# Differential attention: another order of each engine's work within a head, and the last input tile of the output projection behind two weight chunks

## What is computed

```python
def diff_mixer(xn, k, v, w_q, q_gain, lam_params, head_gain, w_out, lambda_init):
    q = rms_norm((xn @ w_q).reshape(B, S, DIFF_HEADS, 2, DIFF_DH), q_gain) * (DIFF_DH ** -0.5)
    lam = jnp.exp(jnp.sum(lp[0] * lp[1])) - jnp.exp(jnp.sum(lp[2] * lp[3])) + lambda_init
    ...
        s = jnp.where(kpos[None, :] <= qpos[:, None], s, -jnp.inf)
        p = jax.nn.softmax(s, axis=-1)
        a = p[:, :, 0] - lam * p[:, :, 1]
        return jnp.einsum('bhqk,bhkv->bhqv', a.astype(v.dtype), v)
    ...
    o = rms_norm(o, head_gain) * (1.0 - lambda_init)
    return o.reshape(B, S, DIFF_HEADS * DIFF_VD) @ w_out
```

## Time and profile before

| | us |
|---|---|
| median of 3 runs | 2490.27 |
| lowest and highest | 2487.11, 2493.24 |
| the profiled execution | 2492.17 |
| its span in the trace | 2490.4 |
| mean granted clock of TensorE, share of full | 0.985 |
| TensorE busy with matmuls | 2395.2 (96% of the span) |
| VectorE busy | 1124.2 (45%) |
| ScalarE busy | 894.8 (36%) |

### The profile page before, as it was taken

One profiled execution on the slowest core, in us unless ns is written; L12 is line 12 of the kernel. 1 busy time (PEld: TensorE's weight loads), 2 busy tenths in 40 slices (PEclk: granted clock), 3 DMA queues, 4 the chain that ended last, 5 costly groups with the idle time before them and its releaser, 6 DMA issues.

```text
span 2490.4 us, 27086 instructions
## 1 busy us (share of the span) xinstructions
PE 2395.2 (96%) x11160; PEld 1928.4 (77%) x11160; DVE 1124.2 (45%) x1744; ACT 894.8 (36%) x1416; POOL 0.2 (0%) x4
## 2 busy tenths in 40 slices
PE   8889999999999999999999889999999997999999
PEld 7556788888877788888788768888887665888887
DVE  4444444344365444344556644324443554542342
ACT  4544332122255322223433433213333664431331
POOL 0000000000000000000000000000000000000000
PEclk9999999999999999999999989999999998999999
DMA  3111222322211222322221112222222110222222
GB/s 128 53 51 68 72 98 83 111 102 79 83 57 62 85 102 87 108 102 82 89 80 60 60 51 97 90 102 102 90 103 85 51 34 34 102 102 86 100 102 85
DMA packets 35579, 206.58 MB, mean 83 GB/s; under 512 B 4080, under 2 KB 4976, under 8 KB 16000
## 3 DMA queue, kind: packets, MB, share of 16 engines
q1 hardware_dynamic: 33120, 199.43, 23.4%
q10 hardware_dynamic: 2336, 5.41, 0.6%
HBM read 202.73 MB, written 2.10 MB: 82 GB/s over the span
## 4 chain that ended last, share of the span: by engine, by line
PE 92%; DVE 4%; ACT 2%; issue 2%; DMA 1%; DVEq 0%; SPq 0%; ACTq 0%
PE ps L285 27%; PE ps L287 27%; PE ps L286 27%; PE ps L980 2%; PE ps L1024 1%; PE ps L1020 1%; PE ps L1890 1%; PE ps L1535 1%; DVE low_w L311 1%; PE ps L1004 1%; PE ps L1871 1%; PE ps L991 1%; DVE diff_p L2097 0%; PE ps L1856 0%; DMA raw_w<-in_w_a_qk 0%
## 5 line engine op out<-in xcount | busy, mean ns | idle before, releaser
L285 PE MATMUL ps<-xh,high_w 128*128 128x512 f32 x1592 | 635.8, 399 | 12.2 <-DVE low_w L330 9.4
L286 PE MATMUL ps<-xl,high_w 128*128 128x512 f32 x1592 | 624.2, 392 | 0.0
L287 PE MATMUL ps<-xh,low_w 128*128 128x512 f32 x1592 | 624.2, 392 | 0.0
L311 DVE TENSOR_TENSOR low_w<-raw_w,high_w 128x2048 fp32r<-128x2048 f32 (+3 forms) x209 | 424.9, 2035 | 204.5 <-ACT high_w L303 204.2
L303 ACT ACTIVATE high_w<-raw_w 128x2048 fp32r<-128x2048 f32 (+3 forms) x209 | 355.2, 1702 | 298.4 <-PE ps L287 281.4
L285 PEld LDWEIGHTS ps<-xh,high_w 128*128 128x128 f32 x1592 | 301.7, 189 | 89.4 <-issue 25.2
L287 PEld LDWEIGHTS ps<-xh,low_w 128*128 128x128 f32 x1592 | 301.4, 189 | 64.3
L286 PEld LDWEIGHTS ps<-xl,high_w 128*128 128x128 f32 x1592 | 301.7, 189 | 61.9 <-issue 1.2
L285 PE MATMUL ps<-ffn_hidh,high_w 128*128 128x512 f32 x864 | 336.1, 389 | 0.0
L286 PE MATMUL ps<-ffn_hidl,high_w 128*128 128x512 f32 x864 | 336.1, 389 | 0.0
L287 PE MATMUL ps<-ffn_hidh,low_w 128*128 128x512 f32 x864 | 336.1, 389 | 0.0
(11 more groups left out here) (241 smaller groups left out, 2581.5 us busy)
## 6 DMA issues: line engine op xcount, KB each, us to landing
raw_w<-in_w_f_gu SPq DMA_DIRECT2D x44, 1024.0 KB, 4.9
raw_w<-in_w_m_up SPq DMA_DIRECT2D x32, 1024.0 KB, 4.9
raw_w<-in_w_m_dn SPq DMA_DIRECT2D x32, 1024.0 KB, 4.9
raw_w<-in_w_f_dn SPq DMA_DIRECT2D x32, 704.0 KB, 4.1
raw_w<-in_w_b_qk SPq DMA_DIRECT2D x8, 1024.0 KB, 4.9
raw_w<-in_w_e_qk SPq DMA_DIRECT2D x4, 1024.0 KB, 4.9
raw_w<-in_w_e_out SPq DMA_DIRECT2D x4, 1024.0 KB, 4.9
raw_w<-in_w_o_q SPq DMA_DIRECT2D x8, 512.0 KB, 3.6
```

The lines of the kernel that those rows point to most:

```text
L285: pe.matmul(out, sh, mh, start=start, stop=False)
L286: pe.matmul(out, sh, ml, start=False, stop=False)
L287: return pe.matmul(out, sl, mh, start=False, stop=stop)
L311: dve.tensor_tensor(wl[slot][:, 0:elems], raw[slot][:, 0:elems], wh[slot][:, 0:elems].bitcast(F32), ALU.subtract).then_inc(w_split, 1)
```

## The change

It changes the order of instructions on TensorE, ScalarE and VectorE within the steps and the tail of the differential attention. `F_BANK` and the counts that go with it are changed. `resid_pe` gets a parameter `late`: with 1, the input tiles 0 to 6 are taken through chunks 0 and 1, and the last tile then through both. Three input tiles of chunk 0 move into head 7's step. On VectorE the masks are cut in two groups with the weight split and the scaling of the next head's Q between them.

```diff
--- before.py
+++ after.py
@@ -604,21 +604,32 @@
         wait_for(pe, R.ready, max(1, k + 1 - R.before))
         return resid_tile(pe, R, c, k)
-    def resid_pe(pe, R, done=0, between={}):
-        def one(c, n):
+    def resid_pe(pe, R, done=0, late=0, between={}):
+        def go(n, k):
+            between.get((n, k), lambda: None)()
             if n == 0:
-                for k in range(done, R.kt):
-                    between.get(k, lambda: None)()
-                    last = resid_first(pe, R, k)
+                last = resid_first(pe, R, k)
             else:
-                pe.wait_ge(w_split, c + 1)
-                banks_read(pe, R, n)
-                for k in range(R.kt):
-                    last = resid_tile(pe, R, c, k)
-            last.then_inc(w_used, 1)
-        each_chunk(R.st, one)
+                if k == 0:
+                    pe.wait_ge(w_split, R.st.base + n + 1)
+                    banks_read(pe, R, n)
+                last = resid_tile(pe, R, R.st.base + n, k)
+            if k == R.kt - 1:
+                last.then_inc(w_used, 1)
+        order = [(0, k) for k in range(done, R.kt)]
+        if late:
+            cut = R.kt - late
+            order = ([(0, k) for k in range(done, cut)] + [(1, k) for k in range(cut)]
+                     + [(0, k) for k in range(cut, R.kt)] + [(1, k) for k in range(cut, R.kt)])
+        for n, k in order:
+            go(n, k)
+        for n in range(2 if late else 1, R.st.count):
+            for k in range(R.kt):
+                go(n, k)
     def resid_act(act, R):
@@ -1763,7 +1774,7 @@
     H = sems("hn", "squared summed logged rooted scaled rounded split")
     NHD = 8
     FQ, FK = (f_q0, f_q1), (f_k0, f_k1)
-    F_BANK = (2, 3, 4, 5, 6, 2, 3, 4)
+    F_BANK = (5, 6, 2, 3, 4, 2, 3, 4)
     def f_probs(buf, i):
         return f_p[:, buf, CAUSAL_AT[i]:CAUSAL_AT[i + 1]]
@@ -1866,7 +1877,7 @@
             for i in rows_of:
                 for hh in range(2):
                     n = 2 * i + hh
-                    wait_past(pe, F["masked"], 8 * p + n - 4 if n > 4 else 8 * (p - 1) + min(n + 6, 8))
+                    wait_past(pe, F["masked"], 8 * p + n - 2 if n > 4 else 8 * (p - 1) + min(n + 4, 8))
                     rows = slice(64 * hh, 64 * hh + 64)
                     pe.matmul(ps[:, F_BANK[n], 0:(i + 1) * P], FQ[st][rows, i * P:(i + 1) * P],
                               FK[st][rows, 0:(i + 1) * P], start=True, stop=True).then_inc(F["scored"], 1)
@@ -1876,7 +1887,7 @@
                 u = TB * p + i
                 pe.wait_ge(F["normed"], u + 1)
                 wait_past(pe, F["pt_copied"], u - 1)
-                pe.wait_ge(F["masked"], clip(8 * (p + 1) + 5, 8 * NHD))
+                pe.wait_ge(F["masked"], clip(8 * (p + 1) + 2, 8 * NHD))
                 for j in range(i + 1):
                     last = pe.transpose(ps[:, T_BANK + i % 2, j * P:(j + 1) * P],
                                         f_probs(st, i)[:, j * P:(j + 1) * P], ident[:, :])
@@ -1907,25 +1918,33 @@
             if past_two(p):
                 head_sum(p - 2)
             scores(p, st, (2, 3))
-            if nx:
-                half(*nx[:2], 1, 0)
             if prev:
                 turn_p(*prev, (0, 1))
             if nx:
-                half(*nx[:2], 1, 1)
+                half(*nx[:2], 1, 0)
+                sums(nx[0], 0)
+            else:
+                resid_first(pe, r_bout, 0)
+                resid_first(pe, r_bout, 1)
             if prev:
                 turn_p(*prev, (2, 3))
             if nx:
-                sums(nx[0], 0)
-                sums(nx[0], 1)
+                half(*nx[:2], 1, 1)
+            else:
+                resid_first(pe, r_bout, 2)
             if prev:
                 pv(prev[0])
+            if nx:
+                sums(nx[0], 1)
+        def before_four(p, st):
+            head_sum(p - 1)
+            turn_p(p, st, (0, 1))
         def tail(p, st):
-            resid_pe(pe, r_bout, 0, {0: lambda: head_sum(p - 1), 2: lambda: turn_p(p, st, (0, 1)),
-                                  3: lambda: turn_p(p, st, (2, 3)), 5: lambda: pv(p),
-                                  7: lambda: head_sum(p)})
+            resid_pe(pe, r_bout, 3, 1, {(0, 4): lambda: before_four(p, st), (0, 5): lambda: turn_p(p, st, (2, 3)),
+                                        (0, 6): lambda: pv(p), (1, 2): lambda: head_sum(p)})
         def project(p, st):
             for which in range(2):
@@ -1988,6 +2007,8 @@
             act.wait_ge(F["pv_done"], p + 1)
             act.wait_ge(F["v_placed"], p + 1)
             stand_alone(act.activation(at_tile(f_vo, p), ps[:, O_BANK, :], ACT.Copy)).then_inc(F["o_taken"], 1)
+        def output_square(p):
             act.wait_ge(F["sums_made"], clip(2 * p + 5, 2 * NHD))
             wait_past(act, H["summed"], p)
             act.activation(sq[:, 0, :], ps[:, O_BANK, :], ACT.Square).then_inc(H["squared"], 1)
@@ -2001,41 +2022,51 @@
             act.wait_ge(H["logged"], p + 1)
             act.activation(sq[:, 2, :], sq[:, 2, :], ACT.Exp, scale=-0.5).then_inc(H["rooted"], 1)
+        def rounded(*tiles):
+            for t in tiles:
+                act.wait_ge(w_used, st_diff.base + NHD)
+                act.wait_ge(H["scaled"], t + 1)
+                act.activation(f_kh[:, t, :], f_vo[:, t, :], ACT.Copy).then_inc(H["rounded"], 1)
         def step(p, st, nx, prev):
             exps(p, st, (0, 1))
             round_weights(act, st_diff.base + p + 2)
+            if nx:
+                square(nx[0], 0)
+            else:
+                rounded(0, 1)
             if past_two(p):
                 head_root(p - 2)
             exps(p, st, (2, 3))
+            if prev:
+                copy_pt(prev[0], (0, 1))
             if nx:
-                square(nx[0], 0)
+                root(nx[0], 0)
+            else:
+                rounded(2)
             if prev:
                 place_values(prev[0])
-                copy_pt(prev[0], range(TB))
+                copy_pt(prev[0], (2, 3))
             if nx:
                 square(nx[0], 1)
-                root(nx[0], 0)
+            else:
+                rounded(3, 4)
+            if prev:
+                output(prev[0])
+            if nx:
                 root(nx[0], 1)
             if prev:
-                output(prev[0])
-        def rounded(t):
-            act.wait_ge(w_used, st_diff.base + NHD)
-            act.wait_ge(H["scaled"], t + 1)
-            act.activation(f_kh[:, t, :], f_vo[:, t, :], ACT.Copy).then_inc(H["rounded"], 1)
+                output_square(prev[0])
         def tail(p, st):
+            copy_pt(p, (0, 1))
             place_values(p)
-            for t in range(0, 3):
-                rounded(t)
-            head_root(p - 1)
-            copy_pt(p, (0, 1))
-            for t in range(3, 5):
-                rounded(t)
             copy_pt(p, (2, 3))
             rounded(5)
+            head_root(p - 1)
             rounded(6)
             output(p)
+            output_square(p)
             head_root(p)
             rounded(7)
@@ -2068,11 +2099,11 @@
                                      in1=sq[:, 2 + which, :], op0=ALU.mult, op1=ALU.mult)\
                .then_inc(F[nm], 1)
-        def mask(p, st):
+        def mask(p, st, rows_of):
             wait_past(dve, F["exped"], 8 * p)
             wait_past(dve, F["normed"], TB * p)
-            for n in range(8):
-                i, hh = n // 2, n % 2
+            for i, hh in [(i, hh) for i in rows_of for hh in range(2)]:
+                n = 2 * i + hh
                 row = 4 * hh + i
                 dve.wait_ge(F["scored"], 8 * p + n + 1)
                 if hh == 0:
@@ -2104,30 +2135,34 @@
             dve.scalar_tensor_tensor(out=at_tile(f_vo, p), in0=at_tile(f_vo, p), scalar=lam[:, 5:6],
                                      in1=sq[:, 2, :], op0=ALU.mult, op1=ALU.mult).then_inc(H["scaled"], 1)
+        def split(*tiles):
+            for t in tiles:
+                dve.wait_ge(H["rounded"], t + 1)
+                dve.tensor_tensor(f_kl[:, t, :], f_vo[:, t, :], f_kh[:, t, :].bitcast(F32), ALU.subtract)\
+                   .then_inc(H["split"], 1)
         def step(p, st, nx, prev):
-            mask(p, st)
+            mask(p, st, (0, 1))
+            split_weights(dve, st_diff.base + p + 2)
             if nx:
                 raw(nx[0], 0)
-            split_weights(dve, st_diff.base + p + 2)
+            mask(p, st, (2, 3))
+            if not nx:
+                split(0, 1)
             if past_two(p):
                 head_scale(p - 2)
             norm(p, st)
             if nx:
+                normed(nx[0], nx[1], 0)
                 raw(nx[0], 1)
-                normed(nx[0], nx[1], 0)
                 normed(nx[0], nx[1], 1)
-        def split(t):
-            dve.wait_ge(H["rounded"], t + 1)
-            dve.tensor_tensor(f_kl[:, t, :], f_vo[:, t, :], f_kh[:, t, :].bitcast(F32), ALU.subtract)\
-               .then_inc(H["split"], 1)
+            else:
```

(7 more changed lines are left out.)

## The result

The changed kernel takes 2507.69 us (median of 4 runs, 2507.32 to 2508.12). The kernel before has 2489.53 us over the 4 runs now shown. The ratio is 1.0072, with a 95% interval of 1.0054 to 1.0089: 18.2 us slower. The forecast was 2500.9 in a range of 2486 to 2508, slower with a chance of 0.54.

A forecast was written before the change was run, and what follows sets the result against it. The prediction took waits, not TensorE's own work, as the bound. Its terms, 2.6+1.5+0.3-5.9+2.4+8.8+0.9 = +10.6 us on 2490.27, gave 2500.9 us; own range 2497 to 2505, wide range 2486 to 2508.

The forecast's parts named there:

- (a): Head steps, TensorE: P times V ahead of K's sum removes the 2.0 us wait in heads with a previous one.
- (b): Score banks: score 7 takes score 4's bank and waits for mask 4; transposes wait for two masks, which frees nothing.
- (c): VectorE's order: split and raw Q precede mask 4, so score 7 starts at T + 11.3 after standing 2.5 us.
- (d): Step length: 22.4 us at full clock; heads 3 to 6 -5.9, heads 0 to 2 +2.6, +1.5, +0.3, head 7 +2.4.
- (e): TensorE's clock behind the new waits: five heads of seven lose it, 1.75 us each, +8.8 us.
- The bounds: Limits set for the clock loss in a step: 0 to 1.8 us.
- (f): Head 7 and projection: 75.4 us for 74.5, +0.9; chunk 2 waits 6.5 us, tile 7's 3.7 us wait goes.
- the clock did not hold: Rival judged: the clock mostly holds, none to three heads lose it, 2492 to 2497 us; chance 0.32.
- the third: Rival: the tail's waits add up and every head loses the clock, +18, 2508 us; chance 0.06.
- The faster rival: Rival: score 7 doesn't wait, mask 4 finished by T + 8.8; steps of 19.85 us, -17, 2473 us; chance 0.12.

The follow-up runs named there:

- the seventh kernel: Changed kernel with masks together, head root and larger exponentials before Q's square, raw K earlier, banks of before, chunk 2 prepared in the tail: 2468.46 us.
- the last experiment: Changed kernel with the sum of Q's squares computed twice in heads 1 to 7: 2510.63 us, ratio 1.0095.
- the third and fourth kernels: Changed kernel with the projection's last input tile in order, 2505.3 us; changed kernel with chunk 2 rounded and split early in the tail, 2498.22 us.
- the first: Changed kernel with VectorE masking all eight score tiles first, then raw Q, then the weight split: 2496.27 us, ratio 1.0037.
- sixth: Changed kernel with masks together, head root and larger exponentials ahead of Q's square, and raw K ahead of the Q tile: 2480.03 us, ratio 0.9961.
- the fifth: Kernel before with only the projection's last input tile taken behind seven tiles of chunk 1: 2491.51 us, ratio 1.0009.

## Why the prediction was right, and where it was off

The mechanism was right: which wait comes, who causes it, and what comes with chunk 2. The size was not. The stage grew by 17.9 us where 10.6 was forecast, and the total is above the forecast's own range of 2497 to 2505. That it still lies within the wide range, by 0.3 us, is in part luck: the changed kernel's profiled stage began 2.1 us earlier than before, which no run ties to the change.

*(a), sums and P times V: right.* K's sum waits in head 0's step alone, 1.4 us, where 1.7 was forecast. In the seventh kernel the same order gives steps of 20.5 us.

*(b) and (c), banks and VectorE's order: right, and shown from both sides.* Score 7 started at T + 11.5 for T + 11.3. Take mask 4 from behind the split, and the wait shrinks from 2.3 to 1.0 us; take the bank from score 7, and the wait moves to the next instruction that needs the mask.

*(d), the step: right within 0.3 us.* 24.2 us with lost clock were forecast as 22.4 plus 1.75; by the last experiment they are 22.7 plus 1.5 to 1.6. Head 0 has 22.5, where 21.1 and 1.75 make 22.9. The wait ahead of head 7's scores was 2.3 for 2.4.

*(e), the clock: the term that was mis-sized.* I took five heads at 1.75, 8.8 us. All seven lost it, and head 5 twice: its step is 25.84, 1.5 above its neighbours, at a PEclk of 0.87. Eight losses of 1.6 make about 12.6, so 3.8 us are missing here, the largest part of the 7.3 that the forecast lacks. The steps' own length is some 2.0 short, the 0.3 of (d) in most heads and more in head 6, and the tail 1.5. The bounds did not hold a second loss in one head. In the third and fourth kernels, whose steps are the same, head 5 loses twice again, and all seven steps agree to 0.03 us. The Trainium skill, "TensorE: Matmul & The Clock Gate", section "Why this matters for your kernels", warns only of gaps longer than these; here waits of 1.8 us lost the clock, so the measurement decides against using it as a safe limit.

*(f), head 7 and the projection: right in its parts.* Score 7 waited 3.9 (forecast 4.5), the first early tile 0.8 (1.1), tile 5 1.9 (2.1), chunk 2 6.4 (6.5), tile 7 nothing. These waits sum to 13.0 for 14.2, yet the stretch grew by 2.4 for 0.9. I kept 5.7 us for slow clock and gaps, and 76.95 less 55.5 and 13.0 leaves 8.4: the saving of 2.4 that I took there did not come, and PEclk is 0.89 for 0.91 before. That tile 7 comes late is a loss only because chunk 2 isn't ready; prepared early, it took 8.7 us off the stage.

The forecast's 10.6 with 3.8, 2.0 and 1.5 makes the 17.9 of the trace. The rivals: the clock did not hold. The tail did not go as badly as in the third, though its other half, every head losing the clock, came true; its 2508, to which I gave 0.06, is nearer to the result than the forecast. The faster rival was wrong in its own terms. Mask 4 by T + 8.8 could not be had by VectorE's order: in the first, sixth and seventh kernels, where nothing of VectorE's stands before it, it ends at T + 9.7. And the score's wait was not the only one. With the masks together the steps are 23.2 us and not 19.85; only ScalarE's order and the banks of before bring them to 20.5. The seventh kernel is faster than before by 20.6 us, but the likeness to the rival's 17 is chance: its steps save 12.4, and the rest is the tail.

## What to carry to other kernels

When an order is written out by hand for several engines, follow the reuse of each buffer through the other engine's queue: a bank that is handed on by a count is free only when everything ahead of that reader has run, a weight split included. Put the readers that release buffers ahead of bulk work that is needed a whole step later. Then look at the whole step again: here the next engine's order was the next limit, and the first repair by itself shortened nothing at full clock. And when a piece of work is pulled behind the next chunk to hide a wait, ask what was prepared in the time that this chunk used to take: here the next chunk's rounding hung on the piece that was put off.

## What the hardware showed that I had not expected

Waits of nearly the same length cost the clock in one head and not in the next: lost after 1.78 us in head 3 of the last kernel and kept after 1.91 in head 4; kept after 2.1 in heads 2 to 4 of the first and lost after 2.1 in its head 5. The kernel before and the fifth have the same steps, and behind the same wait of 2.5 us the one keeps the clock and the other loses it. In the changed kernel it was lost in all seven heads, in one of them twice, and the third and fourth repeat this head by head. A single loss cost 1.4 to 1.8 us. Work of 0.86 us added to each step, with no wait changed, moved the losses to other heads, from eight in the changed kernel to seven.
